# A small buffer is cut from 32 to 8 columns, and every buffer behind it in SBUF starts 96 bytes earlier

## The reference, cut to what matters

```python
def first_block(x, ...):
    mixed = token_mix(rms_norm(x, norm1_g), w_in, ...)    # fox | gdn | hgrn | gla, 256 wide each
    x = x + mixed @ w_out
    x = x + conv_glu_ffn(rms_norm(x, norm2_g), w_up, ffn_conv_w, ffn_conv_b, w_down)
    return x

def conv_glu_ffn(h, w_up, conv_w, conv_b, w_down):        # D_FF = 2816
    u = causal_dwconv(h @ w_up, conv_w) + conv_b
    gate, up = jnp.split(u, 2, axis=-1)
    return (jax.nn.silu(gate) * up) @ w_down

def second_block(x, positions, ...):
    h = x
    h = h + short_conv_mixer(rms_norm(h, g0), conv_w_in, conv_w, conv_w_out)
    h = h + swiglu_ffn(rms_norm(h, g1), w13, w2)
    k_nope, k_pe, v = shared_mla_kv(h, ...)
    h = h + mla_mixer(rms_norm(h, g2), w_dq, q_norm_g, w_uq, w_o, k_nope, k_pe, v, cos, sin)
    h = h + swiglu_ffn(rms_norm(h, g3), w13b, w2b)
    return rms_norm(h, final_norm_g)
```

## Time and profile before

| | |
|---|---|
| median of 3 executions | 2016.1 us (2014.39, 2016.10, 2018.18) |
| the profiled execution's own time | 2018.18 us |
| its span, first to last instruction | 2016.0 us |
| mean granted TensorE clock | 0.983 |
| TensorE matmul busy | 1933.5 us (96%), 8769 instructions |
| VectorE, ScalarE, GpSimd busy | 1011.3, 763.5, 328.4 us |
| DMA moved | 161.23 MB, mean 80 GB/s |

### The profile page before, as it was taken

The page is one execution under the profiler, slowest core; times in us unless marked ns, Lnnn a source line. Parts: engine busy times, 40 slices in busy tenths (PEclk is TensorE's granted clock), DMA queues, the critical chain, the costliest instruction groups (busy, mean ns, idle before and its releaser), DMA issues.

```text
span 2016.0 us, 25343 instructions
## 1 busy us (share of the span) xinstructions
PE 1933.5 (96%) x8769; PEld 1558.1 (77%) x8769; DVE 1011.3 (50%) x1417; ACT 763.5 (38%) x1095; POOL 328.4 (16%) x278
## 2 busy tenths in 40 slices
PE   7989988879999999999999999999999999999998
PEld 6779855556788888888878888888776678888887
DVE  5463478766476775335445434433466544344322
ACT  5532564325444443232234233322355442232222
POOL 0051056540211111010012111110100021111110
PEclk9999999889999999999999999999999999999999
DMA  6310210011233333333333333333322033333332
GB/s 185 84 32 1 53 32 12 21 32 49 87 95 103 95 94 97 95 100 94 94 94 94 94 97 100 91 97 95 98 68 63 16 90 94 102 95 94 95 95 71
DMA packets 309219, 161.23 MB, mean 80 GB/s; under 512 B 12688, under 2 KB 306832, under 8 KB 309024
## 3 DMA queue, kind: packets, MB, share of 16 engines
q1 hardware_dynamic: 308080, 157.64, 27.2%
q0 software_dynamic: 640, 2.17, 0.3%
q10 hardware_dynamic: 432, 0.52, 0.1%
HBM read 158.21 MB, written 2.10 MB: 80 GB/s over the span
## 4 chain that ended last, share of the span: by engine, by line
PE 89%; DVE 4%; ACT 3%; issue 3%; SPq 0%; POOL 0%; DMA 0%; DVEq 0%; ACTq 0%; POOLq 0%
PE ps L365 25%; PE ps L367 25%; PE ps L366 25%; PE ps L1031 2%; PE ps L1019 1%; PE ps L1431 1%; PE ps L1627 1%; PE ps L1452 1%; PE ps L1439 1%; PE ps L1913 1%; PE ps L1914 1%; DVE mx L1488 1%; PE ps L1618 1%; DVE mx L1343 0%; PE ps L876 0%
## 5 line engine op out<-in xcount | busy, mean ns | idle before, releaser
L365 PE MATMUL ps<-xhi,whi 128*128 128x512 f32 x1656 | 664.7, 401 | 10.1 <-DVE xlo L437 6.7
L367 PE MATMUL ps<-xhi,wlo 128*128 128x512 f32 x1656 | 646.9, 391 | 0.0
L366 PE MATMUL ps<-xlo,whi 128*128 128x512 f32 x1656 | 646.9, 391 | 0.0
L352 ACT ACTIVATE whi<-raw 128x1024 fp32r<-128x1024 f32 (+2 forms) x297 | 309.0, 1040 | 715.6 <-PE ps L367 713.3
L360 DVE TENSOR_TENSOR wlo<-raw,whi 128x1024 fp32r<-128x1024 f32 (+2 forms) x293 | 361.8, 1235 | 280.0 <-ACT whi L352 279.9
L365 PEld LDWEIGHTS ps<-xhi,whi 128*128 128x128 f32 x1656 | 312.6, 189 | 82.1 <-issue 4.5
L366 PEld LDWEIGHTS ps<-xlo,whi 128*128 128x128 f32 x1656 | 312.4, 189 | 67.7 <-issue 5.6
L367 PEld LDWEIGHTS ps<-xhi,wlo 128*128 128x128 f32 x1656 | 312.1, 188 | 65.8
L594 DVE TENSOR_TENSOR zS<-ps,rs 128x512 f32<-128x512 f32 x132 | 91.3, 691 | 293.6 <-PE ps L367 284.4
L367 PE MATMUL ps<-h_hi,wlo 128*128 128x512 f32 x528 | 205.4, 389 | 0.0
L365 PE MATMUL ps<-h_hi,whi 128*128 128x512 f32 x528 | 205.4, 389 | 0.0
(11 more groups left out here) (323 smaller groups left out, 1954.2 us busy)
## 6 DMA issues: line engine op xcount, KB each, us to landing
raw<-in_conv_ffn_w SPq DMA_DIRECT2D x52, 512.0 KB, 3.8
raw<-in_mla_ffn_w SPq DMA_DIRECT2D x52, 512.0 KB, 3.8
raw<-in_w_up SPq DMA_DIRECT2D x44, 512.0 KB, 3.8
raw<-in_w_in SPq DMA_DIRECT2D x28, 512.0 KB, 3.8
raw<-in_conv_w_in SPq DMA_DIRECT2D x24, 512.0 KB, 3.7
raw<-in_w_down SPq DMA_DIRECT2D x16, 448.0 KB, 3.5
raw<-in_conv_ffn_w SPq DMA_DIRECT2D x16, 448.0 KB, 3.6
raw<-in_mla_ffn_w SPq DMA_DIRECT2D x16, 448.0 KB, 3.6
```

Source lines behind the costliest of these rows:

```text
L352: a.activation(whi[:, u % PARTS, 0:n], raw[:, u % RAW, 0:n], ACT.Copy).then_inc(hi_split, 1)
L365: t_.matmul(out, wh, xh, start=first, stop=False)
L366: t_.matmul(out, wh, xl, start=False, stop=False)
L367: return t_.matmul(out, wl, xh, start=False, stop=last)
```

## The change

One number in a declaration changes.

```diff
@@ -254,7 +254,7 @@
         rs = sb("rs", [P, T])
         xg = sb("xg", [P, 2, T])
         stat = sb("stat", [P, 4, 4])
-        credit = sb("credit", [P, 32])
+        credit = sb("credit", [P, 8])
         ps = ctx.enter_context(nc.psum_tensor("ps", [P, 8, T], F32))
         NRING = 6
```

## The result

| | before | after |
|---|---|---|
| median | 2017.14 us (4 runs) | 2031.36 us (4 runs) |
| lowest and highest | 2014.39, 2019.52 | 2025.62, 2032.88 |
| span of the profiled execution | 2016.0 us | 2027.6 us |
| TensorE busy | 1933.5 us | 1944.1 us |

The ratio is 1.0065, with a 95% interval from 1.0047 to 1.0085, or 9 to 17 us. The forecast was no change, 2016.1 us, and its range ended at 2022 us. Both were wrong.

What follows compares the result with a forecast made beforehand. TensorE was taken to bound the kernel, at 89% of the chain, with waits between engines in the mixers. Six terms of 0 summed to 0 us, so the median forecast was 2016.1 us, range 2011 to 2022 us.

Steps and rivals of the forecast that it cites:

- Where the time is bound: Whole kernel: TensorE 89% of the chain, no gap in long products; in mixers engines wait for each other.
- TensorE, the moving operand: 1932 float32r passes on moved activations: bounds 0 to 13.7 us, taken as 0 from the half products.
- The rival of one more piece: Down, convolution output and latent products: one more 64 byte piece per row, 13.7 us, plus 4.4 on VectorE and ScalarE; chance 0.09.
- TensorE's weight load: Mixers and attentions: a stationary operand 4 bytes over loads in 227 against 224 ns; taken as 0.
- VectorE: Its 81 us of the chain: shifted operands bounded at -1.1 to +1.2 us; taken as 0.
- ScalarE: Its 60 us of the chain, judged by line 1409's copies: 0.7 us at most; taken as 0.
- GpSimd: Product with a mask in cst: shifted 1243 against 1305 ns; chain share rounds to 0%; taken as 0.
- DMA: Loads of x at the start and stores of fin at the end: 0.3 us by 1 in 32; taken as 0.
- Lines of 16 bytes: All engines: 96 bytes are six SBUF lines, operands keep their place within a line, so the price is nothing.
- The rivals of meeting accesses: VectorE and ScalarE on the path: engines' accesses meet more, 5.3 us slower, chance 0.06; or less, 5.3 us faster, chance 0.11.

Runs made afterwards that it cites:

- e1: Kernel before, with everything in SBUF from xT on starting 32 bytes later, relative places kept: ratio 1.0011, 2018.82 us.
- e9: Kernel before, with only the weights whi and wlo starting 32 bytes later, all other buffers keeping their place modulo 256: ratio 1.0207, 2058.72 us.
- e10: Kernel before, with xhi and xlo 16 bytes later modulo 256, h_hi and h_lo of the first two nets 4 bytes later: ratio 1.0169.
- e12: Changed kernel, with every product's weights cut to their first 64 columns and two banks zeroed once at the start: one run, 2037.59 us.
- e8: Kernel before, with activations, weights, constants and work buffers 32 bytes later modulo 256, raw alone keeping its place: ratio 1.0000.
- e13: Kernel before, with wlo alone starting 32 bytes later, all else keeping its place modulo 256: ratio 1.0203, 41 us slower.
- e11: Kernel before, with credit 8 columns wide and 24 unused columns behind it, so all starts stay: ratio 1.0002, 2017.53 us.
- e3: Kernel before, with padding that puts xhi and xlo at distance 160 from the weights, h passes at 226.7 ns: ratio 1.0171.
- e6: Kernel before, with xhi and xlo 128 bytes later relative to the weights, h_hi and h_lo 256 bytes later: ratio 1.0141.
- e2: Kernel before, with whi and wlo 32 bytes later and all that stands behind them moved by 128 bytes: ratio 1.0201, 2057.08 us.
- e4: Kernel before, with credit 16 columns wide, so mx, h_hi and so on start at an odd multiple of 64 bytes: ratio 1.0070, 2029.46 us.

## Why the prediction was wrong

**Where the time is bound.** Right: TensorE bounds, the long products have no gap, and all of the change came out there.

**TensorE, the moving operand: the step that failed.** It asked what an operand costs that starts 32 bytes over a multiple of 64, found only the half products of rows 5, and took their 0. The measured value is 7.6 ns per pass, 14.7 us. Two things were wrong with the step. The question was wrong: no absolute start costs (e1), the distance to the weights does. And the row did not answer even that. In rows 5 the distance does change, with b, but these are full float32 matmuls, 64 columns in 113 ns; the float32r passes stream 512 columns in 227 ns. The rows at a granted clock of 0.50 bear out that the rate decides: at 427 ns per pass no distance costs anything. The text had noted that a limit could hide there, put 7.1 ns as the upper bound, and then chose the lower end because that row was nearer. With ends 0 and 13.7 us apart and no row at the full rate, 0.09 for the upper end was too little, and the range should have reached it.

**The rival of one more piece.** Its place was right, and its TensorE price of 13.7 us stands within 1.0 us of the passes' 14.7, but its mechanism is wrong, and so the agreement is chance: by it e1 should have cost 54 us and cost 2, and e9, where no activation moved, should have cost nothing and cost 42. Its other part, 4.4 us on VectorE and ScalarE, did not happen.

**TensorE's weight load, VectorE, ScalarE, GpSimd, DMA.** Taken as 0 from pairs of rows, and no price came out. The prediction judged line 1409 by one group of four, and only the move itself, which did not swap them, shows that their difference is no matter of the start. The loads of `xhi` products keep 188 ns, loads of x land in 6.3 us and the stores of `fin` in 2.9 us.

**Lines of 16 bytes.** The Trainium skill's rule on SBUF lines ("SBUF — State Buffer", section "Specifications (TRN2)") priced the change at nothing, since 96 bytes are six lines. The change and e10's 16 bytes, one line exactly, both cost; the rule does not cover what happened here, and the measurement decides.

**The rivals of meeting accesses.** They looked for meetings between engines, which would be felt in the mixers. The runs point to two reads of one engine, the stream and the weights. The profile before had a hint: at a granted clock of 0.50 the passes stood 427 ns apart, half of which is 213.3, and at 1.00 they stood 226.7 ns apart with nothing waiting. That 13 ns was never asked about.

**Open.** How a shifted operand slows its neighbours, why 4 bytes are worst, what the 13 ns at distance 0 are, and why with weights of 64 columns passes at one distance have paces from 226.8 to 233.3 ns (e12). That the distance between stream and weights decides is shown for weights of 128 columns (e1, e8, e9). That it acts through the weight load is inferred: no run takes the load away, as every matmul here has one. In favour are that the pass during which `wlo` is loaded pays most in e13, and that the price is the same with VectorE, ScalarE and GpSimd idle.

## What to carry to other kernels

Declare or pad buffers so that the moving and the stationary operands of fast (here float32r) matmuls start at the same place modulo 256 bytes, and all parts of a split operand alike; here, at the full clock and with weights of 128 columns, that is worth 2 to 5% of the pace of such passes, and up to 2.1% of the kernel. A change of the size of any buffer moves all behind it, so after one compare the distance of starts of the main matmuls, not just the mean length of groups. When a cost is bounded from rows at a lower rate, the range must keep the upper end.

## What the runs showed of the hardware

Pace of float32r passes of 512 columns, weights of 128 columns, at a granted clock of 1.00 (at 0.50 it is 425 to 428 ns at every distance that occurs there), by start of the moving operand minus start of the weights, modulo 256 bytes:

| distance | pace, ns | from |
|---|---|---|
| 0 | 226.7 | before, e1, e8, e11; h in e3, e6 |
| 4 | 238.0 | h in e10 |
| 16 | 231.7 | x in e10 |
| 96 | 233.4 | h in e2 |
| 128 | 232.4 | x in e6 |
| 160 | 234.3 | the change; x in e3 |
| 192 | 233.3 | h in e4 |
| 224 | 233.3 | x in e2 and e9, h in e9 |

The Trainium skill says in "SBUF — State Buffer", section "Who interferes with whom", that TensorE has two independent read ports, one for the stream and one for the weight load, and never waits on anyone. e9 and e13 do not fit the independence: moving nothing but weights by 32 bytes took the passes from 226.7 to 233.3 ns. Full float32 matmuls showed no such price. In line 1031 the change moved both operands, so there only rows 5 speak, with distances of 16, 32 and 64 bytes. In line 1719 it moved the stream (`grow`) against fixed weights (`cst`); 512 columns have 592 ns before and after, and where nothing is waited for, the next matmul starts 429 or 430 ns later, before and after:

```profile
L1719 PE MATMUL ps<-grow,cst 128*128 128x512 f32 x8 | 4.1, 592 | 0.0
```
